# Gated product and sine argument kept in PSUM, the sine ahead of two roundings, one group of key products a projection later

## The reference, cut to what matters

```python
def _swiglu(h, w_gate, w_up, w_down):
    return (jax.nn.silu(h @ w_gate) * (h @ w_up)) @ w_down

# first stack, each layer
x = x + 0.5 * _swiglu(_rmsnorm(x, ffn1_norm[i]), ffn1_w_gate[i], ffn1_w_up[i], ffn1_w_down[i])
...                                   # mixer; in its Hyena filters, three times: sin(freq * (h @ w + b))
x = x + 0.5 * _swiglu(_rmsnorm(x, ffn2_norm[i]), ffn2_w_gate[i], ffn2_w_up[i], ffn2_w_down[i])
# second stack, each layer: mixer, then
x = x + jnp.einsum('bsf,fd->bsd', jax.nn.silu(causal_dwconv(g_ff, w, b)) * u_ff, ffn_out[l])
```

## Time and profile before

| | |
|---|---|
| three executions | 1991.63, 1993.33, 1993.42 us (median 1993.33) |
| the profiled execution, its own time | 1991.4 us |
| its span, first to last instruction | 1989.6 us |
| PE busy | 1952.2 us (98%) |
| DVE, ACT, POOL busy | 956.7 (48%), 1038.4 (52%), 1491.4 us (75%) |
| granted TensorE clock | 0.999 of 2.4 GHz |
| DMA | 329.09 MB, 165 GB/s |

### The profile page before, as it was taken

One profiled execution on the slowest core, in us unless ns is written; L12 is line 12 of the kernel. 1 busy time (PEld: TensorE's weight loads), 2 busy tenths in 40 slices (PEclk: granted clock), 3 DMA queues, 4 the chain that ended last, 5 costly groups with the idle time before them and its releaser, 6 DMA issues. The chain is left out here.

```text
span 1989.6 us, 37005 instructions
## 1 busy us (share of the span) xinstructions
PE 1952.2 (98%) x15763; PEld 1799.0 (90%) x15763; DVE 956.7 (48%) x1605; ACT 1038.4 (52%) x1551; POOL 1491.4 (75%) x652
## 2 busy tenths in 40 slices
PE   7999999999999999999999999999999999999998
PEld 7998788989989998788899989999999899999997
DVE  3560778343305550778343204845585038356750
ACT  5443456464436444456564437455644374656442
POOL 6789455469887889446278887768789877687896
PEclk9999999999999999999999999999999999999999
DMA  6756333136555756333145574545555645455653
GB/s 223 248 181 206 110 107 127 42 114 207 184 199 172 226 183 202 102 107 107 45 149 191 191 231 151 168 149 191 170 191 192 208 155 166 146 190 168 194 197 127
DMA packets 250965, 329.09 MB, mean 165 GB/s; under 512 B 9008, under 2 KB 225586, under 8 KB 250418
## 3 DMA queue, kind: packets, MB, share of 16 engines
q1 hardware_dynamic: 250802, 326.73, 50.6%
HBM read 325.66 MB, written 1.05 MB: 164 GB/s over the span
## 5 line engine op out<-in xcount | busy, mean ns | idle before, releaser
L1020 POOL TENSOR_TENSOR w_lo<-raw,w_hi 128x1024 fp32r<-128x1024 f32 x600 | 1455.7, 2444 | 480.4 <-ACT w_hi L597 478.9
L410 PE MATMUL psA<-xT_hi,w_lo 128*128 128x256 f32 x3168 | 896.3, 283 | 8.1 <-POOL w_lo L1020 4.2
L411 PE MATMUL psA<-xT_lo,w_hi 128*128 128x256 f32 x3168 | 883.8, 279 | 0.0
L412 PE MATMUL psA<-xT_hi,w_hi 128*128 128x256 f32 x3168 | 883.8, 279 | 0.0
L597 ACT ACTIVATE w_hi<-raw 128x1024 fp32r<-128x1024 f32 x600 | 630.3, 1052 | 360.4 <-PE psB L412 237.6
L410 PEld LDWEIGHTS psA<-xT_hi,w_lo 128*128 128x128 f32 x3168 | 599.2, 189 | 22.2 <-issue 11.4
L411 PEld LDWEIGHTS psA<-xT_lo,w_hi 128*128 128x128 f32 x3168 | 595.6, 188 | 2.5 <-issue 2.4
L412 PEld LDWEIGHTS psA<-xT_hi,w_hi 128*128 128x128 f32 x3168 | 597.4, 189 | 0.0
L1166 DVE TENSOR_TENSOR hT_lo<-hfull,hT_hi 128x256 fp32r<-128x256 f32 x132 | 214.8, 1659 | 2.8 <-ACT hT_hi L730 1.4
L410 PE MATMUL psB<-w_hi,hT_lo 128*128 128x512 f32 x528 | 205.6, 389 | 1.4 <-issue 1.4
L412 PE MATMUL psB<-w_hi,hT_hi 128*128 128x512 f32 x528 | 205.5, 389 | 0.0
(11 more groups left out here) (446 smaller groups left out, 2319.3 us busy)
## 6 DMA issues: line engine op xcount, KB each, us to landing
raw<-in_w_in SPq DMA_DIRECT2D x78, 1024.0 KB, 5.1
raw<-in_ffn_w_gate SPq DMA_DIRECT2D x44, 1024.0 KB, 5.1
raw<-in_ffn_w_up SPq DMA_DIRECT2D x44, 1024.0 KB, 5.2
raw<-in_ffn_w_down SPq DMA_DIRECT2D x44, 1024.0 KB, 4.8
raw<-in_w_ffn_in SPq DMA_DIRECT2D x44, 1024.0 KB, 5.0
raw<-in_w_ffn_out SPq DMA_DIRECT2D x22, 1024.0 KB, 4.8
raw<-in_w_out SPq DMA_DIRECT2D x16, 1024.0 KB, 4.8
raw<-in_w_branch_da SPq DMA_DIRECT2D x4, 1024.0 KB, 4.8
```

The lines of the kernel that those rows point to most:

```text
L410: nc.tensor.matmul(o, a_lo, b_hi, start=start, stop=False, skip_group_check=skip)
L411: nc.tensor.matmul(o, a_hi, b_lo, start=False, stop=False, skip_group_check=skip)
L412: return nc.tensor.matmul(o, a_hi, b_hi, start=False, stop=stop, skip_group_check=skip)
L1020: nc.gpsimd.tensor_tensor(split_half(w_lo, n, kind), raw_half(n, kind), split_half(w_hi, n, kind).bitcast(F32), ALU.subtract)\
```

## The change

There are four edits. (1) The product of Silu and up projection is written back into its bank of `psA` and not into `hfull`; ACT rounds it from there, DVE takes the rest from there, and PE may overwrite the bank when the rest has been taken (`f_lo`) and no more when the product was made. DVE's wait for an older rest goes. (2) The sine argument is made in bank 3 of `psB`: the first scaling is done twice (once into `farg`, once in place), and the chain alternates so that each instruction reads one tile of PSUM; the sine reads PSUM. (3) On ACT the sine stands after the second Silu of its step and no more after the last rounding of a product; the down product waits for the third sine and no more for the third argument. (4) The fourth group of key products stands after projection 26.

```diff
 # ACT, ffn
+                    if st == 0 and f == 0 and j in (6, 8, 10):
+                        mlp_sin(l, j // 2 - 3)
                     for i in range(2):
...
                         act.wait_ge(f_prod[st].sem, f_prod[st].due(l, NF * f + n + 1))
-                        A(hT_hi[:, n, :], hfull[:, i, :], ACT.Copy).then_inc(f_hi[st].sem, 1)
-                    if st == 0 and f == 0 and j in (6, 8, 10):
-                        mlp_sin(l, j // 2 - 3)
+                        A(hT_hi[:, n, :], psA[:, 2 + i, 0:L], ACT.Copy).then_inc(f_hi[st].sem, 1)
...
-                A(hdn[:, 1:L + 1], farg[:, 0, :], ACT.Sin).then_inc(s1["mlp_sin"].sem, 1)
+                A(hdn[:, 1:L + 1], psB[0:HID, 3, 0:L], ACT.Sin).then_inc(s1["mlp_sin"].sem, 1)
 # DVE, ffn
-                        if n >= 2:
-                            dve.wait_ge(f_lo[st].sem, f_lo[st].due(l, NF * f + n - 1))
-                        V.tensor_tensor(hfull[:, i, :], sg[:, i, :], psA[:, 2 + i, 0:L], ALU.mult).then_inc(f_prod[st].sem, 1)
+                        V.tensor_tensor(psA[:, 2 + i, 0:L], sg[:, i, :], psA[:, 2 + i, 0:L], ALU.mult).then_inc(f_prod[st].sem, 1)
...
-                        V.tensor_tensor(hT_lo[:, n, :], hfull[:, i, :], hT_hi[:, n, :].bitcast(F32), ALU.subtract)\
+                        V.tensor_tensor(hT_lo[:, n, :], psA[:, 2 + i, 0:L], hT_hi[:, n, :].bitcast(F32), ALU.subtract)\
 # DVE, mlp_argument
-                a, n = farg[:, 0, :], farg[:, 1, :]
+                a, b, n = farg[:, :], psB[0:HID, 3, 0:L], psB[0:HID, 3, L:2 * L]
...
-                V.tensor_scalar(a, psB[0:HID, 3, 0:L], cols[0:HID, 113 + k:114 + k],
-                                                cols[0:HID, 116:117], ALU.add, ALU.mult).then_inc(ch.sem, 1)
+                V.tensor_scalar(a, b, cols[0:HID, 113 + k:114 + k], cols[0:HID, 116:117], ALU.add, ALU.mult)
+                V.tensor_scalar(b, b, cols[0:HID, 113 + k:114 + k], cols[0:HID, 116:117], ALU.add, ALU.mult).then_inc(ch.sem, 1)
...
-                    V.scalar_tensor_tensor(a, n, -c, a, ALU.mult, ALU.add).then_inc(ch.sem, 1)
+                    V.scalar_tensor_tensor(b if c == c3 else a, n, -c, a, ALU.mult, ALU.add).then_inc(ch.sem, 1)
...
-                V.tensor_scalar(a, a, pi, -pi, ALU.min, ALU.max).then_inc(s1["mlp_arg"].sem, 1)
+                V.tensor_scalar(b, b, pi, -pi, ALU.min, ALU.max).then_inc(s1["mlp_arg"].sem, 1)
 # PE, ffn
-                            pe.wait_ge(f_prod[st].sem, f_prod[st].due(l, NF * f + 2 * (j - 1) + i + 1))
+                            pe.wait_ge(f_lo[st].sem, f_lo[st].due(l, NF * f + 2 * (j - 1) + i + 1))
...
-                    pe.wait_ge(s1["mlp_arg"].sem, s1["mlp_arg"].due(l, 3))
+                    pe.wait_ge(s1["mlp_sin"].sem, s1["mlp_sin"].due(l, 3))
 # PE, stack1_projections
                         turn_rows_kv(l, 0)
+                    if i == 26:
                         key_products(l, 3)
-                    if i == 26:
                         turn_rows_kv(l, 1)
```

More of the change, by code:

```diff
@@ L233, in emit @@
         root_row = at("root_row", 98, [P, L])
-        hfull = at("hfull", 46, [P, 2, L])
         xn = at("xn", 87, [P, RB, D])
@@ L254, in emit @@
         hdn = at("hdn", 105.0, [HID, L + 1])
-        farg = at("farg", 102.0, [HID, 2, L])
+        farg = at("farg", 102.0, [HID, L])
         skip = at("skip", 83, [P, 2, HYW])
@@ L1198, in mlp_argument @@
                 c3 = float(np.float32(2 * math.pi - c1 - c2))
-                V.tensor_scalar(a, psB[0:HID, 3, 0:L], cols[0:HID, 113 + k:114 + k],
-                                                cols[0:HID, 116:117], ALU.add, ALU.mult).then_inc(ch.sem, 1)
+                V.tensor_scalar(a, b, cols[0:HID, 113 + k:114 + k], cols[0:HID, 116:117], ALU.add, ALU.mult)
+                V.tensor_scalar(b, b, cols[0:HID, 113 + k:114 + k], cols[0:HID, 116:117], ALU.add, ALU.mult).then_inc(ch.sem, 1)
                 dve.wait_ge(ch.sem, ch.step(l))
-                V.tensor_scalar(n, a, 1 / (2 * math.pi), big, ALU.mult, ALU.add).then_inc(ch.sem, 1)
+                V.tensor_scalar(n, b, 1 / (2 * math.pi), big, ALU.mult, ALU.add).then_inc(ch.sem, 1)
                 dve.wait_ge(ch.sem, ch.step(l))
```

## The result

Four executions of the changed kernel took 1977.63 to 1979.03 us, median 1977.73, beside a median of 1993.38 for the kernel before: ratio 0.9919, 95% interval 0.9903 to 0.9935. The profiled execution took 1977.63 us with a span of 1975.5, 14.1 less than before. The forecast was 1986.0, its range 1983 to 1990.5: the direction was right, and the gain was twice as large as forecast. The forecast's part of it is in the trace almost to the tenth; the other half comes from the pace of PE's matmuls, which the forecast had taken as one number.

A forecast was written before the change was run, and what follows sets the result against it. PE, busy in 98% of the span, was taken as the bound, so only its waits could be won: -7.3 us, key products 0, gives 1984.1 on the profiled execution, 1986.0 on the median; range 1983 to 1990.5.

The forecast's parts named there:

- The waits: PE's waits for POOL's `w_lo` in the first-stack FFNs: all were forecast to go, 7.3 us together.
- the seven places: First stack: four waits in layer 0's first FFN, one in layer 1's, one in each second FFN; 7.3 us.
- 0.42 forecast: DVE's rest `hT_lo`, read from PSUM: 0.42 us each, taken from `hfull`, between bounds of 0.41 and 1.56.
- rival B: DVE's rest `hT_lo` stays held, by its output; only the sine rounds' waits shrink, 3.0 us together: 1990.3; chance 0.08.
- The new wait for the rest: PE's wait before overwriting an up bank: rest done at P + 1.3, PE back after 5.3 us, cover 4 us.
- the 3.0 that was worked out: Edits 2 and 3 alone: the four waits of the sine rounds shrink by 0.6 to 0.8, -3.0 us in waits.
- Rival A: The sine chain becomes the bound; only second steps gain, 2.1 us, or halfway 4.7 us: 1988.6; chance 0.08.
- P + 4.86: P ends a step's last product; the gate after the sine was forecast at P + 5.8, costing PE nothing until P + 7.05.
- The value taken, 0: Key products: their wait goes, 2.1 us in all, but PE then waits for POOL's masks; bounds -2.1 to +1.2.
- What a wait costs: Prediction's step pricing each PE wait as its bracket plus 0.25 us, with matmuls 0.11 us apart; sum 7.3 us.
- rival C: PSUM traffic stretches PE's matmuls: over 4.4% eats the 7.3 us, 10% costs 16.6: 2002.6; chance 0.06.

The follow-up runs named there:

- the first profile: Profiled execution of the changed kernel, 1977.63 us; the second profile is from measuring the changed kernel again, 1977.09 us, ratio 0.9918.

## Why the prediction was right, and where it failed

**The waits** were right in kind, place and size. Aligning PE's instructions before and after, over the late matmul and the two behind it, the seven places give 1.04, 2.63, 0.63, 0.95 and 0.92, 0.54 and 0.54: 7.25 against the forecast 1.04 + 2.63 + 0.63 + 2 x 0.96 + 2 x 0.55 = 7.3. Every term came.

**Edit 1.** 0.42 forecast, 0.421 measured, in all cases. The output stayed fp32r and the POOL work beside it stayed too, so it was the second SBUF input that held `hT_lo`, not the output: rival B is out. The Trainium skill's rule in "SBUF — State Buffer", section "Who interferes with whom" (one SBUF input, no contention with GpSimd), is what this trace shows, with 421 ns where the median was 1558. The new wait for the rest was hidden, as costed.

**Edits 2 and 3.** Alone they gave the 3.0 that was worked out for a kernel with held rests; on top of edit 1 nothing is left for them in the waits (7.3 with edit 1 alone, 7.25 with all four). Rival A is out: the gate comes at P + 4.86, and no wait for `w_lo` is left where the sine is made.

**Edit 4.** PE comes a microsecond earlier and loses it to the masks: it gains 0.95 and 1.17 in the two layers, then loses 0.89 and 1.35. The value taken, 0, was right, and for the reason given.

**The step that failed** is the one under "What a wait costs": "In a steady stretch PE's matmuls start 0.11 us apart", and with it the costing of a wait by its own gap alone. There are two steady paces, and a wait that ends late can also change the pace of what follows. The rows for this stood in the trace of before: after 100.82 the next matmuls start 0.12 apart, not 0.11, up to the next foreign matmul at 112, and at 443.39 a bracket of 0.30 was followed by 862 slow steps, 3.9 us. The range and rival C asked only whether PE could get slower; that a third of the kernel ran 4% under its own best pace was not asked. The missing term is -7.3 us in the first profile and -8.9 in the second (17.1 of excess are left there). Shown is: the second stack's share, 860 slow steps or 3.9 us before, comes from edit 1 in that undoing it there brings the restarts and the slow halves back; and in the FFNs of all profiles the pace changes only at interruptions. Edit 1 does not secure it: with edit 1 alone the last FFN was slow from its entry on, behind a late matmul that the changed kernel has too (at 1801.43) and that left PE fast there. Not settled: which interruption leaves which pace, and why there are two. That the missing term had the sign of the forecast gain was luck: nothing in the forecast bore on it. So how much of the first stack's share any one edit earns is not shown: there the entries of the FFNs, which the change touches only in their timing, turned the pace both ways (the second FFN of layer 0 was fast at its entry before and slow after).

## What to carry to other kernels

Don't price a stall by its gap alone: compare the start-to-start step of equal matmuls before and behind it, and count how many run at the slower one. Print the number of matmuls in equal windows over the whole span first; two numbers where there should be one is a term for the sum, and it may hang on a wait of 0.01 us that no list shows. And when executions of one kernel spread by several us at one granted clock (edit 1 alone: 1976.8 to 1987.2), look for such a state before looking for a cause in the edit; that the pace makes this spread is likely but not shown, since the trace of one execution of it is on record.

## What the runs showed of the hardware that was not expected

- At a granted clock of 1.00, fp32r matmuls of 256 columns, each with its own weight load, start 113.3 or 117.9 ns apart, slow for up to 1006 steps on end; those of 512 columns show one pace, 227 ns.
- In the FFNs of these runs the pace changes only at an interruption of PE's own stream. A foreign fp32 matmul of 128 or 256 columns without a wait swaps it (119 of 125); its own cost is 0.25 or 0.43 us. A restart leaves it slow in 44 of 54 cases.
- DVE's subtraction with an fp32r output takes 421 ns from PSUM beside a busy POOL, and 410 to 2628 with both inputs in SBUF.
